# Branch merge in plain fp32, and merge, output projection, norm and queries in one stage

## What is computed

```python
y_conv = c @ conv_pw2                      # c: 640 x 1024, conv_pw2: 1024 x 2048
o = o * rsqrt(mean(o*o)) * dn_norm_g * silu(z)
y_dn = o @ dn_w_o                          # o: 640 x 1024, dn_w_o: 1024 x 2048
g_conv, g_dn = split(sigmoid(gates), 2)
out = (g_conv * y_conv + g_dn * y_dn) @ w_out      # w_out: 2048 x 2048
x = x + out
xn = rms_norm(x, norm_ffn_g)
q = xn @ peer_w_q                          # 2048 x 2048, then product-key top-16 per head
...
x = x + peer(xn, ...)                      # 8 heads x 16 experts of 16384
y = rms_norm(x, norm_final_g)
```

## Time and profile before

| | us |
|---|---|
| median of 3 runs | 5491.55 (5487.92 to 5493.11) |
| the profiled execution, its own time | 5483.01 |
| its span, first to last instruction | 5481.4 |
| stage m, from SyncE's first load to its last store | 1851.0 to 2137.0 |
| stage o, the same | 2142.2 to 2445.2 |
| stage q, the same | 2455.4 to 2791.4 |
| last stage | from 2797.0 |

### The profile page before, as it was taken

The page is one execution under the profiler, slowest core; times in us unless marked ns, Lnnn a source line. Parts: engine busy times, 40 slices in busy tenths (PEclk is TensorE's granted clock), DMA queues, the critical chain, the costliest instruction groups (busy, mean ns, idle before and its releaser), DMA issues. The chain is left out here.

```text
span 5481.4 us, 72178 instructions
## 1 busy us (share of the span) xinstructions
PE 5044.8 (92%) x23597; PEld 3848.4 (70%) x23597; DVE 3057.8 (56%) x3905; ACT 896.3 (16%) x1389; POOL 973.9 (18%) x778
## 2 busy tenths in 40 slices
PE   7999998999999597969944999999999999999996
PEld 5555555877777496967734877777777777777774
DVE  1465653333332123026875777777777777777776
ACT  1111112111110111110057111111111111111110
POOL 0000000000000032310000333333332233333321
PEclk8999999999999798989978999999999999999998
DMA  2111112111121435232149999989899999989896
GB/s 103 65 63 59 62 52 72 51 51 51 61 78 51 162 134 199 77 137 101 38 109 160 362 343 345 343 342 347 334 351 350 349 345 344 344 340 345 343 346 245
DMA packets 351115, 1103.77 MB, mean 201 GB/s; under 512 B 154704, under 2 KB 183760, under 8 KB 263632
## 3 DMA queue, kind: packets, MB, share of 16 engines
q1 hardware_dynamic: 276176, 562.54, 29.9%
q0 software_dynamic: 74752, 538.99, 25.8%
HBM read 1027.84 MB, written 73.59 MB: 201 GB/s over the span
## 5 line engine op out<-in xcount | busy, mean ns | idle before, releaser
L1784 PE MATMUL ps<-aT,work 128*128 128x384 f32 x4096 | 1368.8, 487 | 21.9 <-DVE aT L1893 20.3
L1784 PEld LDWEIGHTS ps<-aT,work 128*128 128x128 f32 x4096 | 773.3, 190 | 506.4 <-issue 36.0
L1768 PE MATMUL ps<-xhi,whi 128*128 128x384 f32 x2048 | 758.7, 370 | 25.6 <-ACT whi L1829 25.4
L411 PE MATMUL ps<-arena 128*128 128x320 f32 x2560 | 714.4, 434 | 1.8 <-issue 1.2
L1769 PE MATMUL ps<-xlo,whi 128*128 128x384 f32 x2048 | 685.8, 335 | 0.0
L365 PE MATMUL ps<-arena 128*128 128x512 f32 x1280 | 657.0, 595 | 7.7 <-DVEq L776 7.7
L1887 DVE TENSOR_TENSOR wlo<-work,whi 128x1024 fp32r<-128x1024 f32 x256 | 313.6, 1225 | 611.6 <-ACT whi L1829 549.3
L1973 POOL DMA_INDIRECT work<-in_peer_u,cur_u x256 | 415.0, 1621 | 1258.9 <-DVE hid L1920 1255.1
L411 PEld LDWEIGHTS ps<-arena 128*128 128x128 f32 x2560 | 478.8, 191 | 192.0 <-issue 11.1
L1829 ACT ACTIVATE whi<-work 128x1024 fp32r<-128x1024 f32 x256 | 271.5, 1060 | 2055.9 <-DMA work<-in_u_units 1998.5
L1930 DVE SCALAR_TENSOR_TENSOR rows<-work,act_w,rows 128x2048 f32<-128x2048 f32 x256 | 600.7, 2347 | 3.1 <-DMA work<-in_peer_v,cur_v 2.6
(11 more groups left out here) (291 smaller groups left out, 5021.7 us busy)
## 6 DMA issues: line engine op xcount, KB each, us to landing
work<-in_u_units SPq DMA_DIRECT2D x256, 512.0 KB
work<-in_v_units SPq DMA_DIRECT2D x256, 512.0 KB
arena<-in_w_group SPq DMA_DIRECT2D x40, 1024.0 KB, 4.8
arena<-in_w_units SPq DMA_DIRECT2D x40, 1024.0 KB, 4.9
gates_dram<-work SPq DMA_DIRECT2D x8, 3072.0 KB, 21.1
gbuf<-gates_dram SPq DMA_DIRECT2D x128, 192.0 KB
m_raw<-in_w_units SPq DMA_DIRECT2D x17, 1024.0 KB, 4.8
o_raw<-in_w_units SPq DMA_DIRECT2D x17, 1024.0 KB, 4.8
```

The lines of the kernel that those rows point to most:

```text
L411: m = pe.matmul(ps[0][:, half * 512:half * 512 + HT], homes[r][:, k, :], xnT[:, k, half * HT:half * HT + HT], start=k == 0, stop=k == KD - 1)
L1768: pe.matmul(out, h3[:, k, :], xhi[:, 8 * half + k, :], start=half == 0 and k == 0, stop=False)
L1784: mmi = pe.matmul(out, w4[:, q, e, :], aT[:, (1 - par) * ET + e, :], start=e == 0, stop=e == ET - 1)
```

## The change

Stages m, o and q become one stage `d`. `c` and `o` are no longer split and the merge multiplies in plain fp32: 32 matmuls a unit instead of 96. The merged row stays on chip: VectorE adds it into `mrow`, ScalarE rounds it straight into `mhi`, VectorE subtracts into `mlo`. `mT_spill` is gone, and so are two stage ends. The gate `z`, `c` and `o` are loaded in quarters, with the first weight unit ahead of them. All three parts share one ring of 2 weight buffers. The last column block of the projection (two units) is computed tile by tile. Square root and scaling are made per tile, and the transposed rows are copied from PSUM straight into `x2`, from which the queries multiply; ScalarE copies the even halves, VectorE the odd ones. `xT_spill` keeps only the 384 tokens that the last stage reads. The core of the diff:

```diff
@@ sync
+            load(0, 0)
+            load_pieces(sp, cz, cT_spill, c_in)
+            for k in range(4):
+                sp.dma_start(piece(of, k), piece(oT_spill, k)).then_inc(o_in[k], 16)
+                sp.dma_start(piece(zf, k), gates_T[2 * KD + 2 * k:2 * KD + 2 * k + 2].rearrange("a p n -> p a n")).then_inc(z_in[k], 16)
+            load(1, 1)
...
+            with sp.Fori(0, MN // 2 - 1) as i:
+                for r in range(2):
+                    st.count(sp, "sp", m_mm, 2 * i + r + 1)
+                    load(2 * i + (r + 2), r)
+                    st.count(sp, "sp", mg_out, 2 * i + r + 1)
+                    gates(2 * i + (r + 2), r)
...
+            with sp.Fori(0, EN // 2) as i:
+                for r in range(2):
+                    st.count(sp, "sp", w_lo, 2 * i + r + 1)
+                    load(2 * i + (MN + 2 + r), r)
...
@@ tensor
-                    units.products(pe, i, r, [(ps[a], NC, chi, clo), (ps[a + 1], H, ohi, olo)], TCOLS)
+            def merge(i, r, first):
+                st.count(pe, "pe", unit_ld[r], 16 * i + 16)
+                if not first:
+                    st.count(pe, "pe", mg_out, 2 * i + r - 1)
+                w3 = ring[r][:].rearrange("p (k c) -> p k c", c=P)
+                for j, x in enumerate((cz, of)):
+                    for k in range(8):
...
+                        for o, c in TCOLS:
+                            m = pe.matmul(ps[2 * r + j][:, o:o + c.stop - c.start], w3[:, 8 * j + k, :], x[:, k, c], start=k == 0, stop=k == 7)
+                m.then_inc(m_mm, 1)
...
+            pe.sem_inc(w_done, 2)
+            pe.wait_ge(m_lo, 8)
+            pe.wait_ge(mg_out, MN)
+            with pe.Fori(0, NOC - 1) as oc:
...
+            for t in range(TILES):
+                pe.wait_ge(wo_add, (NOC - 1) * TILES + t + 1)
+                for kh in range(2):
+                    wh, wl = weights(kh)
+                    pe.wait_ge(w_hi, EN - 1 + kh)
+                    high(t, kh, wh)
+                    pe.wait_ge(w_lo, EN - 1 + kh)
+                    m = low(t, kh, wl)
+                m.then_inc(wo_mm, 1)
+            pe.wait_ge(wo_add, NOC * TILES + TILES)
...
+            pe.wait_ge(n_evac, 2 * TILES)
@@ scalar
-            split_hi(act, cz, chi, c_in, 16, c_hi)
-            split_hi(act, of, ohi, o_scaled, 1, o_hi)
+            with act.Fori(0, MN - 1) as n:
+                merged(n)
+            weight(0, 0)
+            merged(MN - 1)
+            weight(1, 1)
...
+            for t in range(TILES):
+                act.wait_ge(wo_add, TILES * (NOC - 1) + t + 1 + TILES)
+                act.activation(junk, x1[:, t, :], ACT.Square, accum_out=nsm[:, 0, t:t + 1]).then_inc(n_sq, 1)
+                act.wait_ge(n_ms, t + 1)
+                act.activation(nsm[:, 2, t:t + 1], nsm[:, 1, t:t + 1], ACT.Sqrt).then_inc(n_root, 1)
+            for t in range(TILES):
+                act.wait_ge(n_tr, 2 * t + 1)
+                if t:
+                    act.wait_ge(n_evac, 2 * t)
+                act.activation(x2[:, 0:8, t * P:(t + 1) * P], ps8(2 * t % 4), ACT.Copy).then_inc(n_evac, 1)
@@ vector
+                    v.tensor_tensor(mrow, gin[r][:, 0, :], gin[r][:, 1, :], ALU.add).then_inc(mg_out, 1)
+                    st.count(v, "dve", mg_out, n + 1)
+                    st.count(v, "dve", m_hi, n + 1)
+                    lo, hi = (w[:, bass.ds(n, 1), :].rearrange("p a t -> p (a t)") for w in (mlo, mhi))
+                    v.tensor_tensor(lo, mrow, hi.bitcast(F32), ALU.subtract).then_inc(m_lo, 1)
...
+            for t in range(TILES):
+                v.wait_ge(n_sq, t + 1)
+                v.tensor_scalar(nsm[:, 1, t:t + 1], nsm[:, 0, t:t + 1], 1.0 / D, EPS, ALU.mult, ALU.add).then_inc(n_ms, 1)
+                v.wait_ge(n_root, t + 1)
+                v.reciprocal(nsm[:, 3, t:t + 1], nsm[:, 2, t:t + 1]).then_inc(n_rs, 1)
+                v.wait_ge(n_rs, t + 1)
+                v.wait_ge(x1_out[t], 16)
+                v.scalar_tensor_tensor(x1[:, t, :], x1[:, t, :], nsm[:, 3, t:t + 1], gain, ALU.mult, ALU.mult).then_inc(n_done, 1)
+            for t in range(TILES):
+                v.wait_ge(n_tr, 2 * t + 2)
+                v.wait_ge(n_evac, 2 * t + 1)
+                v.tensor_copy(x2[:, 8:16, t * P:(t + 1) * P], ps8((2 * t + 1) % 4)).then_inc(n_evac, 1)
@@ gpsimd
+            with pool.Fori(0, EN // 2) as i:
+                for r in range(2):
+                    st.count(pool, "pool", w_hi, 2 * i + r + 1)
+                    st.count(pool, "pool", w_done, 2 * i + r + 1)
+                    pool.tensor_tensor(wlo[:, r, :], ring[r][:], whi[:, r, :].bitcast(F32), ALU.subtract).then_inc(w_lo, 1)
```

More of the change, by code:

```diff
@@ L1041, in build @@
         first.close()
[L1043 to L1103, removed]
@@ L1357, in build @@
-        units.stream(block, 2 * NOC)
-        st.end()
-        st = Stage("q")
-        x2 = st.sb("x2", [P, KD, T])
-        RING = 4
-        ring = [st.sb(f"ring{i}", [P, UW]) for i in range(RING)]
-        BASE = H + 3 * KD + 2 * NOC
-        qa = st.sb("qa", [P, KD * T])
+        st = Stage("d")
+        MN, EN, QN = KD, 2 * NOC, HP
+        M0, E0, Q0 = H + 2 * KD, H + 3 * KD, H + 3 * KD + 2 * NOC
+        rows3 = st.sb("rows3", [P, 3 * NC * T])
+        ring = [st.sb(f"ring{i}", [P, UW]) for i in range(2)]
@@ new lines, in _ @@
+            load(1, 1)
+            for k in range(2):
+                sp.wait_ge(o_scaled[k], 1)
+                gates(k, k)
+            with sp.Fori(0, MN // 2 - 1) as i:
[4 more added lines that the diff above has]
+                    gates(2 * i + (r + 2), r)
+            for n in range(MN - 2, MN):
+                sp.wait_ge(m_mm, n + 1)
+                load(n + 2, n % 2)
@@ new lines, in _, with weights, high @@
+            for r in range(2):
+                merge(0, r, True)
+            with pe.Fori(1, MN // 2) as i:
+                for r in range(2):
+                    merge(i, r, False)
+            def weights(kh):
+                return tuple(w[:, kh, :].rearrange("p (k c) -> p k c", k=8) for w in (whi, wlo))
+            def high(t, kh, wh):
+                for k in range(8):
+                    for x in (mhi, mlo):
+                        m = pe.matmul(oc_bank(t), x[:, 8 * kh + k, t * P:(t + 1) * P], wh[:, k, :], start=kh == 0 and k == 0 and x is mhi, stop=False)
@@ L1448, in query @@
                     if k == 4 and not (first and r == 0):
[L1449 removed]
+                        if first:
                             pe.wait_ge(key_ld, 16)
[L1451 removed]
+                        scores(j - 1, 1 - r)
                     for o, c in TCOLS:
[L1453 to L1454 removed]
@@ L1455, in _ @@
-            for r in range(RING):
+                        m = pe.matmul(ps[r][:, o:o + c.stop - c.start], w3[:, k, :], x2[:, k, c], start=k == 0, stop=k == KD - 1)
+                m.then_inc(q_mm, 1)
+            for r in range(2):
                 query(0, r, True)
-            with pe.Fori(1, HP // RING) as i:
-                for r in range(RING):
+            with pe.Fori(1, QN // 2) as i:
+                for r in range(2):
                     query(i, r, False)
-            scores(HP - 1, 1)
+            scores(QN - 1, 1)
@@ new lines, in _ @@
+            v.sem_inc(wo_add, TILES)
+            v.wait_ge(xr_ld, 32)
+            with v.Fori(0, NOC) as oc:
+                for t in range(TILES):
+                    st.count(v, "dve", wo_mm, oc * TILES + t + 1)
+                    part = x1[:, t, bass.ds(oc * OCW, OCW)]
+                    v.tensor_tensor(part, part, oc_bank(t), ALU.add).then_inc(wo_add, 1)
+            v.wait_ge(g_ld, 16)
+            for t in range(TILES):
+                v.wait_ge(n_sq, t + 1)
[5 more added lines that the diff above has]
+                v.scalar_tensor_tensor(x1[:, t, :], x1[:, t, :], nsm[:, 3, t:t + 1], gain, ALU.mult, ALU.mult).then_inc(n_done, 1)
```

360 lines of the change are left out of this document (125 added, 235 removed).

## The result

The changed kernel takes **5447.42 us** (median of four runs, 5445.34 to 5448.26) against 5490.44 us for the kernel before on the same chip: ratio 0.9918, 95% interval 0.9903 to 0.9933. It is 43 us faster. Run again on another occasion beside five variants it gave 5443.76 against 5489.33, ratio 0.9915 (0.9901 to 0.9928). The profiled execution took 5447.09 us, span 5445.5.

A forecast was written before the change was run, and what follows sets the result against it. TensorE was taken to bound merge and projection, with three idle seams around them; 44.6 us won by the queries' start less 2.4 at the end gave - 42.2, from the median 5491.55 to 5449 us, range 5434 to 5466.

The forecast's parts named there:

- Head and merge: Stage start and merge: first product at 1857.8 instead of 1889.06, 17.23 us a unit, merge end at 2137.7 against 2130.7.
- rival 3: Merge: plain fp32 costs four whole passes, 18.8 us a unit, + 24 us, 5473 us; chance 0.05.
- Seam to the projection: From merge end (E) to first projection product: GpSimd's subtraction holds VectorE's last add; start at 2145.0 instead of 2164.85.
- E + 7.3: TensorE's projection start after merge end E if GpSimd wins the lock, 2145.0; E + 2.9 if VectorE wins.
- Projection: First product to last add: 245.3 us against 244.0, with + 1.6 us waiting for a low part in the last block.
- Norm and copies: Last add to first query product: scalings behind all adds, then copies in turn; 28.6 us instead of 54.7.
- 4.4 + 4 x 3.1: Norm after the last add: 4.4 us for the first tile, 3.1 for each further one, 16.8 us in all.
- Queries and end: Last part of the merged stage: queries unchanged; clearing 61 semaphores instead of 25 at the end costs + 2.4 us.
- 1: Seam to the projection: VectorE wins the lock, TensorE starts at E + 2.9; 5445 us, chance 0.34.
- 2: Norm overlaps the last column block after all, T (last add) + 16 instead of T + 28.6; 5437 us, chance 0.03.
- 4: Merge: TensorE's granted clock falls, gain gone at 0.86, 5708 us at half clock; chance 0.03 with all other slower ways.
- 5: Seams shrink but a new wait of 35 us or more replaces them; 5484 us, about no change; chance 0.03.

The follow-up runs named there:

- the late rounding: Changed kernel, with TensorE waiting for its own last merge product before it tells ScalarE that the first projection unit may be rounded: 5446.95 us.
- another order: Changed kernel, with the last column block's adds taken out of VectorE's loop and each row tile's norm right behind the next tile's add: 5438.65 us, ratio 0.9908.

## Why the prediction was right, point by point

The direction, the range and the likeliest case held. The closeness of 5449 to 5447 is partly luck: by its own thread the sum was 6.6 us short (48.8 us won at the start of the last stage, 42.2 forecast), and this was hidden because the profiled execution of before, from which I started, had a last stage some 10 us shorter than usual, while I moved the sum to the median by 8.5.

- **Head and merge: right.** 1857.23 for 1857.8, a unit of 17.2 us, end at 2137.5 for 2137.7. The price of plain fp32 from the rows of the first stage held to 0.1%, and rival 3 (18.8 us a unit) fell. The Trainium skill (FP8 and Floating Point Precision, TensorE Precision Notes) says four passes for true fp32; in time a plain product costs 3.7 reduced ones here (0.541 us against 0.147).
- **Seam to the projection: mechanism half right, 2.3 us off.** The step that failed is "GpSimd then starts its subtraction at E + 1.6 to E + 2.2". It started 2.4 us ahead of E: the counter step in TensorE's program released ScalarE at 2132.85, while products that stand in front of it were still being made. So the add went almost free, and another wait, named nowhere in the prediction, set the start: the counter step of L1381 behind the last subtraction. Moving it showed that (5.04 to 3.35 us). With the late rounding GpSimd started at E + 2.4, near the time that the prediction gave it, and even then the add went first and free; the subtraction behind it was held (8.03). That GpSimd holds the add until its own end plus 0.7 us, the premise of "E + 7.3", came about in neither of these runs, since the add began either in GpSimd's last 0.3 us or before it.
- **Projection: right.** 244.97 us for 245.3, with the forecast stall in the last block:

```profile
2362.67 1.22 PE L1230 MATMUL ps<-d_wlo,d_mhi 128*128 128x256 f32 x8 [1.50 <-POOL d_wlo L1508]
```

- **Norm and copies: mechanism right, 2.7 us too long.** 25.86 us for 28.6. The mis-sized term is "4.4 + 4 x 3.1": it measured 14.4 us, not 16.8, the first tile 2.9 and each further one 2.88. ScalarE loaded its table far ahead of the mean:

```profile
2366.68 1.28 ACT L1332 ACT_TABLE_LOAD   x1
...
2387.69 0.20 ACT L1332 ACTIVATE d_nsm<-d_nsm 128x1 f32<-128x1 f32 x1 [19.73 <-DVE d_nsm L1392]
```

In the kernel before the same load began only behind the mean (2415.37), and the prediction took that over; why it stands ahead here is open. That VectorE's order lets nothing but squares be hidden held to the letter: with or without the tile-by-tile form it is 25.86 us, with another order 18.31. The copies in turn took 11.4 us for 11.8.
- **Queries and end: right.** 326.4 us from first product to the last store's issue, 327.5 before; from there to the next stage 8.36 us for 5.97, + 2.4 as forecast from the earlier trace rows. The row of after that answers:

```profile
L1034 SPq DRAIN  x2: 7/7/7, 1842.3 to 2743.6; - x2
...
L1034 POOLq DRAIN  x2: 40/40/41, 1850.5 to 2747.9; - x2
```

- **Rivals.** 1 (VectorE's add free) is nearest to what happened, at E + 5 and not E + 2.9: its price left out L1381, and with that step moved the start came at 3.2 to 3.4 us. 2 did not occur, and the run with another order shows it needed just that. 4 did not: 0.99 in the merge. 5 did not.

## What to carry to other kernels

When a stage is merged into its neighbour, follow for each engine not only the data but each bare counter step: where it stands in the program decides, since on TensorE it can run ahead of queued products and on VectorE it waits its turn behind work nobody needs. A tile-by-tile order on one engine hides nothing while the next engine's program still takes all tiles of one step before the first of the next; compare both orders before paying for it. And price a change of stages from the starts of stages: what one profiled execution shows for a 2700 us stage of gathers can be 10 us off its usual length.

## What I had not expected of the hardware

- A counter step in TensorE's program was seen 4.7 us ahead of the end of the products in front of it (ScalarE released at 2132.85, products done by 2137.58); waiting for the products' own counter moved ScalarE's start to 0.07 us behind VectorE's (2139.84 and 2139.77).
- The first 6 us of the queries ran at a granted clock of 0.72 in the changed kernel and at 1.00 where the norm lay in the last block; first product to last store was 326.38 and 324.70 us, the 1.7 us named above. With the changed kernel's norm but the copies side by side, or with the last block in the loop, it was 324.69 and 324.67 too, and the first 6 us ran at 1.00 there as well. So the 1.7 us go with the granted clock, and the place of the norm is not what decides that; what does is open.

```profile
2413.45:2419.45 6.00, 6.00 (x16) 4.03 (x17) 0.12 (x1) 0.00 (x0) 0.00 (x0) 0.72 0.83 298
```

and the same stretch of the run with the norm in the last block:

```profile
2404.05:2410.05 6.00, 6.00 (x23) 4.26 (x23) 0.12 (x1) 0.00 (x0) 0.00 (x0) 1.00 0.82 297
```
